# Expert loop: slot 3 in the first slot's buffer, slots 3 and 4 fetched before the router's tables, two low parts made by GpSimd

## The chip, the core and the metric

The kernel runs on one core of one Trainium2 chip. The metric is the device time of one execution in microseconds (us), as the median of several runs.

## What is computed

Two transformer blocks over 512 tokens of width 1024, in float32. The first block has sparse latent attention, a chunked gated MLP and a mixture of experts; the second has dilated attention, forgetting attention and SwiGLU layers. The change touches the mixture of experts only:

```python
def hier_moe(h, ...):
    # group = top 1 of 4, then top 2 of its 8 experts; comb = gate weights, zero elsewhere
    y = zeros_like(h)
    for e in range(32):
        he = silu(h @ w_gate[e]) * (h @ w_up[e])      # 1024 -> 256
        y = y + comb[:, e:e + 1] * (he @ w_down[e])   # 256 -> 1024
    return y
```

## The kernel before, in words

The 1024 pairs of token and expert are sorted by expert into slots of up to 64 rows. A slot belongs to one expert. The first 32 slots are those of experts 0 to 31, in order, whatever the router finds; experts with more than 64 rows get further slots behind them. Here 36 slots are worked off, one after the other.

Products are made in a split form. A weight w is parted into a high part (rounded by ScalarE) and a low part (w minus the high part, a subtraction of two operands in SBUF); TensorE multiplies by both. For a slot, ScalarE makes `up_high` and VectorE `up_low` (line 2553) from the gate and the up weights in two steps (q = 0 gate, q = 1 up), each 128x2048. They are double buffered by the slot's parity. `m_low` counts the low parts: 1 and 2 are slot 0's, 3 and 4 slot 1's, 2j + 1 and 2j + 2 slot j's.

Raw weights come by transfers of 1 MB for gate, up and down, issued in program order by SyncE (lines 672, 675, 678). Slot 0's stand in `w_first`; all later slots use a ring of two buffers, odd slots in one and even slots in the other. The gate and up transfers of slot j wait until slot j - 2's low parts are made, its down transfer until slot j - 2's down product is done. Slots 0, 1 and 2 are fetched before the router; slots 3 and 4 follow once the router's tables are there (`rt_tables`), since `next_up` reads the expert's number from a table.

The router runs between the rows' norm and the loop, at about 395 to 412 us: VectorE does some 60 small steps (compare, multiply, reduce; most wait for the step before), with short products on TensorE between. It writes `slot_rows` (which rows a slot has) and the trip count. GpSimd then gathers each slot's rows by indirect transfers and scatters the results. `keep_clock` issues idle products on TensorE so that its clock is kept.

In a period of the loop VectorE adds the two halves of the gated product (line 2280), multiplies by the Silu, copies the down product of an earlier slot out of PSUM, and makes the two low parts of the next slot with a step for its rows between. The first of these periods stand written out ahead of the loop.

Before the loop VectorE makes slot 0's gate low part ahead of the router (at 391.8), its up low part right behind the tables (at 412.0), and both of slot 1's behind the first rows. GpSimd clears the gather buffer `xg` at 369 and then waits for `slot_rows`.

## Time and profile before

| | us |
|---|---|
| median of 3 runs | 2420.23 |
| lowest, highest | 2414.74, 2420.58 |
| the profiled execution | 2420.1 |
| its span, first to last instruction | 2418.2 |

| engine | busy us | share of the span |
|---|---|---|
| TensorE | 2305.2 | 95% |
| VectorE | 979.5 | 41% |
| ScalarE | 968.9 | 40% |
| GpSimd | 945.1 | 39% |

All times inside the kernel are in us from the start of the span. PE is TensorE, DVE VectorE, ACT ScalarE, POOL GpSimd, SP SyncE; SPq is SyncE's issuing of a transfer. The shares hold for the whole kernel; the stage that the change touches runs from about 395 to 730 us, and there the windows, the waits and the timeline have to be read for themselves. `L2553` is line 2553 of the kernel. A row of the timeline gives start, duration, engine, line, operation, output and inputs, shapes and count.

### The profile page before, as it was taken

To read this page: it belongs to the slowest core of one execution; us is meant where nothing else is said; L and a number is where in the kernel's file an instruction comes from. 1 tells how busy PE (TensorE), PEld (TensorE's weight loads), DVE (VectorE), ACT (ScalarE), POOL (GpSimd) and SP (SyncE) were. 2 spreads that over 40 slices of the span, in tenths; PEclk is the share of its full clock that TensorE was granted. 3 is DMA by queue.
4 is the path that set the end of the run, shared out by engine and by line. 5 is a ranking of instruction groups with operands and counts; after the bars stand their busy time and mean duration, and the time that the engine had idled before them with its cause. 6 is when DMAs were issued, how large, how long until landed. Compare 5 with 4: busy or idle time off the path is not lost.

```text
span 2418.2 us, 31089 instructions
## 1 busy us (share of the span) xinstructions
PE 2305.2 (95%) x11628; PEld 1872.7 (77%) x11628; DVE 979.5 (41%) x1631; ACT 968.9 (40%) x1611; POOL 945.1 (39%) x757
## 2 busy tenths in 40 slices
PE   7999998888888999999998899999999999999998
PEld 6886786444446998899987778888878887888887
DVE  4377445888884233363335621111321124211113
ACT  3344523666663344343343432222344444322223
POOL 4441241535552433333332145454432222544542
PEclk9999999999999999999999999999999999999999
DMA  5521146999983422312322133333232211233332
GB/s 180 170 76 47 40 156 226 356 391 399 387 322 116 146 84 96 102 53 70 105 86 73 36 92 101 99 93 105 88 106 87 70 53 53 87 105 91 101 98 85
DMA packets 210268, 316.25 MB, mean 131 GB/s; under 512 B 20640, under 2 KB 140192, under 8 KB 200304
## 3 DMA queue, kind: packets, MB, share of 16 engines
q1 hardware_dynamic: 202416, 301.98, 36.5%
q0 software_dynamic: 7744, 12.76, 1.6%
q8 instruction: 76, 1.25, 0.2%
q14 instruction: 32, 0.26, 0.0%
HBM read 300.89 MB, written 22.71 MB: 134 GB/s over the span
## 4 chain that ended last, share of the span: by engine, by line
PE 77%; DVE 6%; issue 5%; DMA 5%; ACT 3%; POOL 2%; SPq 1%; DVEq 0%; ACTq 0%; POOLq 0%
PE bank L873 21%; PE bank L875 21%; PE bank L874 21%; DMA w_ring<-in_w_gate 4%; PE bank L1493 2%; PE bank L1125 2%; POOL w_low L3036 2%; DVE up_low L2553 2%; PE bank L912 1%; PE bank L1104 1%; PE bank L1470 1%; PE bank L1115 1%; PE bank L1480 1%; ACT up_high L1984 1%; PE bank L1297 1%
## 5 line engine op out<-in xcount | busy, mean ns | idle before, releaser
L3036 POOL TENSOR_TENSOR w_low<-raw,w_high 128x512 fp32r<-128x512 f32 x568 | 743.4, 1340 | 1180.7 <-ACT w_high L1730 1148.8
L873 PE MATMUL bank<-h_high,w_high 128*128 128x512 f32 x1088 | 430.8, 396 | 2.3 <-DVE h_low L2297 2.3
L875 PE MATMUL bank<-h_high,w_low 128*128 128x512 f32 x1088 | 425.5, 391 | 0.0
L874 PE MATMUL bank<-h_low,w_high 128*128 128x512 f32 x1088 | 425.1, 391 | 0.0
L1730 ACT ACTIVATE w_high<-raw 128x2048 fp32r<-128x2048 f32 x145 | 276.9, 1909 | 246.8 <-PE bank L875 233.8
L873 PE MATMUL bank<-w_high,h_high 128*128 128x512 f32 (+2 forms) x832 | 328.2, 394 | 13.6 <-ACT qk L2065 4.1
L875 PE MATMUL bank<-w_high,h_low 128*128 128x512 f32 (+2 forms) x832 | 312.3, 375 | 0.0
L874 PE MATMUL bank<-w_low,h_high 128*128 128x512 f32 (+2 forms) x832 | 312.3, 375 | 0.0
L873 PEld LDWEIGHTS bank<-h_high,w_high 128*128 128x128 f32 x1088 | 205.3, 189 | 47.1 <-DVE h_low L2297 6.1
L875 PEld LDWEIGHTS bank<-h_high,w_low 128*128 128x128 f32 x1088 | 205.0, 188 | 43.6
L874 PEld LDWEIGHTS bank<-h_low,w_high 128*128 128x128 f32 x1088 | 205.3, 189 | 40.4
L873 PEld LDWEIGHTS bank<-w_high,h_high 128*128 128x128 f32 x832 | 204.9, 246 | 29.3 <-DVE h_low L2297 4.6
L875 PEld LDWEIGHTS bank<-w_high,h_low 128*128 128x128 f32 x832 | 204.9, 246 | 12.3
L874 PEld LDWEIGHTS bank<-w_low,h_high 128*128 128x128 f32 x832 | 206.1, 248 | 10.7
L2553 DVE TENSOR_TENSOR up_low<-w_ring,up_high 128x2048 fp32r<-128x2048 f32 x70 | 160.2, 2290 | 25.2 <-ACT up_high L1984 24.4
L2277 DVE TENSOR_TENSOR gu<-silu,bank 128x512 f32<-128x512 f32 x44 | 30.3, 688 | 321.4 <-ACT silu L2177 321.4
L2177 ACT ACTIVATE silu<-bank 128x512 f32<-128x512 f32 x44 | 26.3, 598 | 333.1 <-PE bank L875 333.1
L2280 DVE TENSOR_TENSOR X<-bank,X 128x512 f32<-128x512 f32 x96 | 65.8, 690 | 210.5 <-PE bank L875 210.2
L1984 ACT ACTIVATE up_high<-w_ring 128x2048 fp32r<-128x2048 f32 x70 | 133.8, 1913 | 23.9 <-DMA w_ring<-in_w_gate 20.7
L2119 ACT ACTIVATE dsc<-dsc,nmx 128x128 f32<-128x128 f32 (+1 forms) x192 | 81.8, 428 | 138.9 <-DVE nmx L2910 138.9
L873 PE MATMUL bank<-w_high,act_high 128*128 128x512 f32 x352 | 136.9, 389 | 0.0
L874 PE MATMUL bank<-w_low,act_high 128*128 128x512 f32 x352 | 136.9, 389 | 0.0
(378 smaller groups left out, 3371.3 us busy)
## 6 DMA issues: line engine op xcount, KB each, us to landing
raw<-in_ffn_w_gu SPq DMA_DIRECT2D x88, 512.0 KB, 4.5
raw<-in_a_w_in SPq DMA_DIRECT2D x72, 512.0 KB, 4.6
w_ring<-in_w_gate SPq DMA_DIRECT2D x35, 1024.0 KB, 10.1
w_ring<-in_w_up SPq DMA_DIRECT2D x35, 1024.0 KB, 12.3
w_ring<-in_w_down SPq DMA_DIRECT2D x35, 1024.0 KB, 9.2
raw<-in_ffn_w_down SPq DMA_DIRECT2D x40, 512.0 KB, 4.6
raw<-in_w_in SPq DMA_DIRECT2D x34, 512.0 KB, 4.6
raw<-in_b_w_in SPq DMA_DIRECT2D x24, 512.0 KB, 4.6
```

The source lines that it names most:

```text
L873: pe.matmul(out, sta[0], mov[0], start=start, stop=False)
L874: pe.matmul(out, sta[0], mov[1], start=False, stop=False)
L875: return pe.matmul(out, sta[1], mov[0], start=False, stop=stop)
L1125: last = pe.matmul(G[qt % 2][:, h * DH:(h + 1) * DH], pt_[:, u % deep, kt * P:(kt + 1) * P], v_[:, kt, h * DH:(h + 1) * DH], start=(kt == ...
L1493: last = pe.matmul(G[t % 2][:, h * DH:(h + 1) * DH], dPT[:, u % 3, o:o + P], dV[:, v % 2, kt, h * DH:(h + 1) * DH], start=(z == 0), stop=( ...
L1730: act.activation(w_high[:, slot, :], raw[:, slot, :], ACT.Copy).then_inc(high_done, 1)
L1984: act.activation(up_high[:, b, :, FE * q:FE * q + FE], ring[:, q, :].rearrange("p (k n) -> p k n", k=KD), ACT.Copy).then_inc(m_high, 1)
L2119: last = act.activation(dsc[:, u % 3, e * w:(e + 1) * w], dsc[:, u % 3, e * w:(e + 1) * w], ACT.Exp, bias=nmx[:, col:col + 1], accum_out=s ...
L2277: return dve.tensor_tensor(out=out, in0=x, in1=y, op=ALU.mult)
L2280: return dve.tensor_tensor(out=out, in0=x, in1=y, op=ALU.add)
L2553: dve.tensor_tensor(out=up_low[:, b, :, FE * q:FE * q + FE], in0=ring[:, q, :].rearrange("p (k n) -> p k n", k=KD), in1=up_high[:, b, :, F ...
L3036: last = pool.tensor_tensor(out=w_low[:, slot, cols], in0=raw[:, slot, cols], in1=w_high[:, slot, cols].bitcast(F32), op=ALU.subtract)
```

## The change

Slot 3 goes to `w_first`, which slot 0 leaves; the ring's two buffers change places (slots 1, 4, 6, 8, ... in ring 0, slots 2, 5, 7, ... in ring 1). SyncE issues the gate and up transfers of slots 3 and 4 by their fixed expert numbers before it waits for the tables, each behind a low part that frees its place; slots 3, 4 and 5 have issues of their own, and the broadcast of `final_norm_g` comes behind slot 6's. GpSimd makes the up low part of slot 0 and the gate low part of slot 1, each in four subtractions of 128x512, while the router runs; VectorE then makes one low part (slot 1's up) after the tables. The router's scratch tiles move to other addresses (two of them over `xg`, with a wait for its clearing), four semaphores of the router become two counting ones, and the first slots of TensorE's and ScalarE's loops are written out.

```diff
-    row_hot = at("row_hot", 93, [P, 2 * NT, R])
-    slot_hot = at("slot_hot", 95, [P, 2 * NT, SLOTS])
+    row_hot = at("row_hot", 29, [P, 2 * NT, R])
+    slot_hot = at("slot_hot", 31, [P, 2 * NT, SLOTS])
...
-    w_ring = [at("w_ring0", AR, [P, 3, 2048]), at("w_ring1", AR + 56, [P, 3, 2048])]
+    w_ring = [at("w_ring0", AR + 56, [P, 3, 2048]), at("w_ring1", AR, [P, 3, 2048])]
...
-        gate(w_ring[1], 1, m_up[1][0])
-        up(w_ring[1], 1, m_up[1][1])
+        gate(w_ring[0], 1, m_up[0][0])
+        up(w_ring[0], 1, m_up[0][1])
...
-                gate(w_ring[0], 2, m_up[0][0])
-                up(w_ring[0], 2, m_up[0][1])
-                down(w_ring[0], 2, m_dn[0])
+                gate(w_ring[1], 2, m_up[1][0])
+                up(w_ring[1], 2, m_up[1][1])
+                down(w_ring[1], 2, m_dn[1])
         sp.wait_ge(rt_out, NT)
-        down(w_ring[1], 1, m_dn[1])
+        down(w_ring[0], 1, m_dn[0])
+        sp.wait_ge(m_low, 1)
+        gate(w_first, 3, m_gate3)
+        sp.wait_ge(m_low, 2)
+        up(w_first, 3, m_up3)
+        sp.wait_ge(m_low, 3)
+        gate(w_ring[0], 4, m_up[0][0])
+        sp.wait_ge(m_low, 4)
+        up(w_ring[0], 4, m_up[0][1])
...
-        next_up(3, 1)
-        next_up(4, 0)
         sp.wait_ge(m_down, 1)
+        down(w_first, 3, m_dn3)
+        sp.wait_ge(m_low, 5)
+        gate(w_ring[1], 5, m_up[1][0])
+        sp.wait_ge(m_low, 6)
+        up(w_ring[1], 5, m_up[1][1])
+        sp.wait_ge(m_down, 2)
+        down(w_ring[0], 4, m_dn[0])
+        next_up(6, 0)
+        sp.wait_ge(m_low, 8)
         sp.dma_start(gw1[:, :], a["final_norm_g"].partition_broadcast(P)).then_inc(gains_loaded, 16)
-        with sp.Fori(2, n_less) as i:
+        with sp.Fori(3, n_less) as i:
             next_down(2 * i - 1, 1)
             next_up(2 * i + 1, 1)
             next_down(2 * i, 0)
...
-        down(0, 0, 1, lambda: rows_come(1, 2))
-        with pe.Fori(1, n_trips) as i:
-            turn_rows(2 * i + 1, 1)
-            up(2 * i, 0, 2 * i - 1)
-            down(2 * i - 1, 1, i, lambda: rows_come(0, i + 2))
...
+        down(0, w_first, m_first, 48, lambda: rows_come(1, 2))
+        turn_rows(3, 1)
+        up(2, 0, 1)
+        down(1, w_ring[0], m_dn[0], 16, lambda: rows_come(0, 3))
...
+        down(3, w_first, m_dn3, 16, lambda: rows_come(0, 4))
...
+        with pe.Fori(2, n_less) as i:
...
+        act.wait_ge(rt_tables, 1)
         rows_high(0, 0)
-        act.wait_ge(rt_tables, 1)
...
-        period(1, 1, 1)
-        with act.Fori(1, n_less) as i:
-            period(2 * i, 0, i + 1)
-            period(2 * i + 1, 1, i + 1)
+        period(1, 1, w_ring[1], m_up[1], 1)
+        period(2, 0, w_first, [m_gate3, m_up3], 1)
+        period(3, 1, w_ring[0], m_up[0], 2)
+        with act.Fori(2, n_less) as i:
...
+        dve.wait_ge(m_idx, 6)
         step(dve.tensor_tensor(out=row_hot[:, :, :],
...
         dve.drain().then_inc(m_y, 1)
-        dve.wait_ge(m_part, 8)
-        up_part(w_first, 0, 1)
+        dve.wait_ge(m_low, 3)
+        up_next(1, 1, 1, w_ring[0])
         rows(0, 0)
         rows(1, 1)
-        up_next(1, 1, 0)
-        up_next(1, 1, 1)
-        period(1, 1)
+        period(1, 1, ring=w_ring[1])
...
-        period(2, 0, 0)
+        period(2, 0, 0, w_first)
...
         pool.memset(xg[:, :, :], 0.0).then_inc(m_idx, 6)
...
+        def up_low_part(ring, b, q):
+            for k in range(0, KD, 2):
+                part = (slice(0, P), b, slice(k, k + 2), slice(FE * q, FE * q + FE))
+                last = pool.tensor_tensor(out=up_low[part],
+                                          in0=ring[:, q, FE * k:FE * k + 2 * FE].rearrange("p (k n) -> p k n", k=2),
+                                          in1=up_high[part].bitcast(F32), op=ALU.subtract)
+            last.then_inc(m_low, 1)
+
+        pool.wait_ge(m_part, 8)
+        pool.wait_ge(m_low, 1)
+        up_low_part(w_first, 0, 1)
+        pool.wait_ge(rt_out, NT)
+        pool.wait_ge(m_high, 1)
+        up_low_part(w_ring[0], 1, 0)
         pool.wait_ge(rt_slots, 1)
```

## Rows read from the trace of the kernel before

**Rows 1.** Page, part 4: shares of the chain by line
```profile
PE bank L873 21%; PE bank L875 21%; PE bank L874 21%; DMA w_ring<-in_w_gate 4%; PE bank L1493 2%; PE bank L1125 2%; POOL w_low L3036 2%; DVE up_low L2553 2%; PE bank L912 1%; PE bank L1104 1%; PE bank L1470 1%; PE bank L1115 1%; PE bank L14
```

**Rows 2.** Windows of the expert stage: window, length, busy us (count) by engine, PEclk, DMA share, GB/s
```profile
core 0: us, PE busy (x) PEld busy (x) DVE busy (x) ACT busy (x) POOL busy (x), PEclk, DMA share, GB/s
395.00:405.00 10.00, 8.26 (x30) 3.87 (x29) 8.94 (x37) 5.71 (x6) 0.00 (x0) 0.90 0.92 366
405.00:412.00 7.00, 4.62 (x20) 2.98 (x21) 4.87 (x19) 0.00 (x0) 1.20 (x2) 0.50 0.00 1
420.00:440.00 20.00, 17.66 (x89) 10.78 (x88) 17.98 (x22) 12.64 (x14) 6.08 (x6) 1.00 0.77 262
440.00:460.00 20.00, 17.85 (x84) 10.55 (x82) 19.08 (x23) 14.23 (x17) 14.93 (x11) 1.00 0.97 378
500.00:600.00 100.00, 83.44 (x382) 48.05 (x380) 86.07 (x93) 61.68 (x68) 51.68 (x46) 0.97 1.01 397
```

**Rows 3.** Waits of ScalarE, 464 to 710 us: line, awaited, us, times, longest
```profile
ACT up_high L1984 <- DMA w_ring<-in_w_gate: 20.7, 23, 1.9
```

**Rows 4.** SyncE issues of ring weights by tile, each with its time to landing
```profile
L672 SPq DMA_DIRECT2D w_ring<-in_w_gate x1: 346/346/346, 421.7 to 421.7; - x1
...
DMA to landing us min/median/max: 4.9/4.9/4.9
...
L678 SPq DMA_DIRECT2D w_ring<-in_w_down x1: 383/383/383, 438.8 to 438.8; - x1
...
DMA to landing us min/median/max: 5.4/5.4/5.4
...
L678 SPq DMA_DIRECT2D w_ring<-in_w_down x1: 391/391/391, 454.6 to 454.6; - x1
...
DMA to landing us min/median/max: 7.6/7.6/7.6
...
L672 SPq DMA_DIRECT2D w_ring<-in_w_gate x1: 333/333/333, 455.9 to 455.9; - x1
...
DMA to landing us min/median/max: 10.2/10.2/10.2
```

**Rows 5.** Timeline of GpSimd and VectorE: the same subtraction with and without GpSimd at work
```profile
1032.69 5.04 POOL L3036 TENSOR_TENSOR w_low<-raw,w_high 128x512 fp32r<-128x512 f32 x4 [17.85 <-ACT w_high L1730]
...
1034.11 1.15 DVE L2853 TENSOR_TENSOR top<-m,msm 128x8 f32<-128x8 f32 x1
1035.30 1.23 DVE L2283 TENSOR_TENSOR mw<-msm,top 128x24 f32<-128x24 f32 x1
...
1053.14 0.18 DVE L2283 TENSOR_TENSOR mw<-msm,top 128x24 f32<-128x24 f32 x1
```

**Rows 6.** Tile w_first and the timeline of VectorE, ScalarE and GpSimd through the router
```profile
L1955 ACT ACTIVATE up_high<-w_first x8: 618/622/622, 387.4 to 394.8; 128x512 fp32r<-128x512 f32 x8
...
395.52 0.17 DVE L2578 TENSOR_TENSOR goh<-logit,rv 128x16 f32<-128x16 f32 x1
...
398.44 0.19 DVE L2573 TENSOR_REDUCE rv<-el 128x4 f32<-128x32 f32 x1
...
411.61 0.16 DVE L2677 CAST trips<-posf 1x3 int32<-1x3 f32 x1
...
410.49 1.01 POOL L3088 DMA_INDIRECT xg<-d_rows,slot_rows  x1 [39.68 <-DVE slot_rows L2666]
```

**Rows 7.** Timeline of VectorE and ScalarE in the first slots of the expert loop
```profile
419.22 4.49 DVE L2553 TENSOR_TENSOR up_low<-w_ring,up_high 128x2048 fp32r<-128x2048 f32 x2
...
423.62 0.74 DVE L2280 TENSOR_TENSOR gated<-lower,bank 64x256 f32<-64x256 f32 x2
...
422.60 1.28 ACT L2007 ACT_TABLE_LOAD   x1
...
440.39 0.74 DVE L2280 TENSOR_TENSOR gated<-lower,bank 64x256 f32<-64x256 f32 x2
...
448.21 0.74 DVE L2280 TENSOR_TENSOR gated<-lower,bank 64x256 f32<-64x256 f32 x2
```

More of the change, by code:

```diff
@@ L197, in two_blocks_kernel @@
     x_turn = at("x_turn", 93, [P, KD, T])
-    row_hot = at("row_hot", 93, [P, 2 * NT, R])
-    slot_hot = at("slot_hot", 95, [P, 2 * NT, SLOTS])
-    cut7 = at("cut7", 97, [P, 2 * NT, T // R - 1])
-    slote = at("slote", 97.25, [1, SLOTS])
-    cnt = at("cnt", 97.5, [1, 1])
-    over = at("over", 97.625, [P, 2 * NT])
-    own = at("own", 97.6875, [P, 2 * NT])
-    cut = at("cut", 97.75, [P, 2 * NT])
-    posf = at("posf", 97.8125, [P, 2 * NT])
-    row_of = at("row_of", 97.875, [P, 2 * NT])
-    starts = at("starts", 98, [P, NE])
-    more = at("more", 98.125, [NE, T // R - 1])
-    more_sum = at("more_sum", 98.1875, [NE, 1])
-    more_wide = at("more_wide", 98.25, [NE, P])
+    row_hot = at("row_hot", 29, [P, 2 * NT, R])
+    slot_hot = at("slot_hot", 31, [P, 2 * NT, SLOTS])
+    cut7 = at("cut7", AR + 28.375, [P, 2 * NT, T // R - 1])
+    slote = at("slote", AR + 28.625, [1, SLOTS])
+    cnt = at("cnt", AR + 28.84375, [1, 1])
+    over = at("over", AR + 28.875, [P, 2 * NT])
+    own = at("own", AR + 28.90625, [P, 2 * NT])
+    cut = at("cut", AR + 28.9375, [P, 2 * NT])
+    posf = at("posf", AR + 28.96875, [P, 2 * NT])
+    row_of = at("row_of", AR + 29, [P, 2 * NT])
+    starts = at("starts", AR + 29.03125, [P, NE])
+    more = at("more", AR + 29.1875, [NE, T // R - 1])
+    more_sum = at("more_sum", AR + 29.21875, [NE, 1])
+    more_wide = at("more_wide", AR + 29.25, [NE, P])
     logit = at("logit", AR + 24, [P, NT, 36])
@@ L1239, in _ @@
         keep_clock(4, TB[0])
-        pe.wait_ge(rt_both, 1)
+        pe.wait_ge(rt_ready, 1)
         for q in range(NT):
             last = pe.matmul(SB[1][0:NE, 0:8], both[:, q, :], ones_r[:, 0:8], start=(q == 0), stop=(q == NT - 1))
-        last.then_inc(rt_cnt, 1)
+        last.then_inc(rt_counted, 1)
         for t in range(NT):
@@ L1298, in up, with down @@
             last.then_inc(m_gu, 1)
-        def down(j, b, uses, come=None):
+        def down(j, ring, loaded, count, come=None):
             pe.wait_ge(m_het, j + 1)
-            if isinstance(j, int) and j == 0:
-                pe.wait_ge(m_first, 48)
-                w = w_first[:, 2, :].rearrange("p (k n) -> p k n", k=2)
-            else:
-                pe.wait_ge(m_dn[b], 16 * uses)
-                w = w_ring[b][:, 2, :].rearrange("p (k n) -> p k n", k=2)
+            pe.wait_ge(loaded, count)
+            w = ring[:, 2, :].rearrange("p (k n) -> p k n", k=2)
             pe.wait_ge(m_y, j + 1)
@@ L1985, in up_part, with up_next @@
                            ACT.Copy).then_inc(m_high, 1)
-        def up_next(j, b, uses, q):
-            act.wait_ge(m_up[b][q], 16 * uses)
+        def up_next(j, b, ring, loaded, uses, q):
+            act.wait_ge(loaded[q], 16 * uses)
             if q == 0 and (not isinstance(j, int) or j >= 2):
                 act.wait_ge(m_gu, j - 1)
-            up_part(w_ring[b], b, q)
+            up_part(ring, b, q)
         def rows_high(j, b):
@@ L2601, in _ @@
         step(add(oh_sum[:, :, :], oh[:, 0, :, :], oh[:, 1, :, :]))
-        spread(both[:, :, :], oh_sum[:, :, :]).then_inc(rt_both, 1)
+        spread(both[:, :, :], oh_sum[:, :, :]).then_inc(rt_ready, 1)
         for k in range(2):
@@ L2696, in inner, with up_next @@
             mul(he[:, :], sg[:, :], gated[:, FE:2 * FE]).then_inc(m_he, 1)
-        def up_next(j, b, q):
+        def up_next(j, b, q, ring):
             dve.wait_ge(m_high, 2 * j + q - 1)
-            up_part(w_ring[b], b, q)
+            up_part(ring, b, q)
         def out(j, b, i):
@@ L2707, in out, with period @@
             dve.tensor_copy(y_out[:, b, 512:1024], G[3][R:2 * R, :]).then_inc(m_y, 1)
-        def period(j, b, i=None):
+        def period(j, b, i=None, ring=None):
+            ring = w_ring[1 - b] if ring is None else ring
             inner(j - 1, 1 - b)
@@ L2712, in period @@
                 out(j - 2, b, i)
-            up_next(j + 1, 1 - b, 0)
+            up_next(j + 1, 1 - b, 0, ring)
             rows(j + 1, 1 - b)
-            up_next(j + 1, 1 - b, 1)
+            up_next(j + 1, 1 - b, 1, ring)
         dve.drain().then_inc(m_y, 1)
-        dve.wait_ge(m_part, 8)
-        up_part(w_first, 0, 1)
+        dve.wait_ge(m_low, 3)
+        up_next(1, 1, 1, w_ring[0])
         rows(0, 0)
         rows(1, 1)
-        up_next(1, 1, 0)
-        up_next(1, 1, 1)
-        period(1, 1)
+        period(1, 1, ring=w_ring[1])
         dve.wait_ge(rt_tables, 1)
```

69 lines of the change are left out of this document (40 added, 29 removed).

## Prediction

> **What bounds the kernel now.** I read the page's chain of waits first: three quarters of it is TensorE in the dense layers, and the expert stage shows up as 4% on the gate weights of the ring [rows 1]. The change touches only the router and the expert loop, 395 to 730 us, so I read that stage by its own views. In the windows the DMA share is 0.92 in the router's first ten us, 0.00 from 405 to 412, 0.77 from 420 to 440, 0.97 to 460, and 1.01 in the loop [rows 2]. The waits of ScalarE say the same: behind 464 us it waited 23 times for a slot's gate weights, 20.7 us in all [rows 3]. So the loop has two speeds. Up to slot 6 VectorE sets the pace, busy 19.08 us of 20 [rows 2], one slot in 7.8 us (gated halves at 440.39 and 448.21 [rows 7]). From slot 7 on the transfers do: its gate weights were issued at 455.9 and landed 10.2 us later, at 466.1 [rows 4]. The end of the loop is the end of that stream of transfers, and what ran dry before is what could be won: the queue is empty while the router works out its tables, which end at 411.61 + 0.16 = 411.8 [rows 6], and the first ring issue after them is at 421.7 [rows 4].
>
> **The change, part by part.**
> *Slots 3 and 4 ahead.* Their experts are numbers 3 and 4 whatever the router finds, so the transfers need no table. The first slot's buffer is free for slot 3 when its two low parts are made, ring 0 (now slot 1's) for slot 4 when slot 1's are. Four transfers of 1 MB move forward: gate 3 to 395, up 3 and gate 4 to GpSimd's two ends (below, 400.7 and 405.8), up 4 behind VectorE's one low part after the tables. At the 397 GB/s of the loop [rows 2] one takes 1.049 MB / 397 = 2.64 us. They are hidden in the empty stretch. Yet the head start does not last: slot 6 still needs slot 4's low parts gone, as before, so the third buffer helps once. I follow the queue, first with the router's end unmoved. Down 3, gate 5, up 5 go out at 429 to 431, when before gate 4 and up 4 did; down 4 at 438; gate 6 and up 6 at slot 4's low parts (the second ends where the gated half at 448.21 starts [rows 7], the first some 2.8 us before, at 445.4); then the broadcast of the norm gains, 0.5 MB, which used to run in a gap behind up 4 and now stands in the way for 1.3 us. Up 6 lands alone, 4.9 us after its issue as gate 3 did [rows 4], at 453.1; the gains at 454.5. Down 5 waits for slot 3's down product and is issued at 454.5, as before [rows 4], so the queue is empty again there. It then lands after 5.4 us, the time of down 3 on an empty queue [rows 4], so at 459.9 or, with the start of the chain 0.2 us earlier, 459.7; before it landed at 454.6 + 7.6 = 462.2. That is 2.5 us won. Gate 7, one transfer behind, lands at 462.4 instead of 466.1: 3.7 us. From here on the stream is full in both kernels, slot for slot the same, and the lead stays. I take 3.1 us, the middle of 2.5 and 3.7. The other ends: 0 if the queue's order eats it, and 4 x 2.64 = 10.6 us if all four transfers that moved ahead come off the end.
> *VectorE's work moved.* After the tables it did one low part of slot 0 and, from 419.22, both of slot 1 (4.49 us) before the first gated half at 423.62 [rows 7]. Now it does one, of slot 1, right after the tables. But ScalarE starts to load its Silu table at 422.60 for 1.28 us [rows 7], so the activation can't start before 423.88, and the next conversion follows it. The cover is the table load: 4.49 us of work go, about 0.2 us of time come back. Ends 0 and 1.0 (423.62 - 422.60).
> *GpSimd's two low parts.* It had nothing to do from 371 to 410 (idle 39.68 before its first gather [rows 6]), so its own time costs nothing. Each low part is four subtractions of 128x512, 5.04 us for four [rows 5]. They begin when ScalarE's last first part is done, 394.8 + 0.62 = 395.4 [rows 6], say 395.5, and run with a small gap to about 405.7. Exactly there VectorE runs the router's chain, dependent step by dependent step. Here the trace has a price: with four such GpSimd subtractions running from 1032.69 on, VectorE's 128x8 and 128x24 subtractions took 1.15 and 1.23 us; the same 128x24 one with GpSimd idle took 0.18 [rows 5]. Each waited out the GpSimd instruction in front of it, and GpSimd was hardly slowed (5.04 / 4 = 1.26). So one dependent two-operand step of VectorE passes per GpSimd instruction. The Trainium skill's page "SBUF — State Buffer", section "Who interferes with whom", states this as an exclusive lock held for a whole instruction, taken when VectorE has two SBUF inputs and GpSimd reads SBUF, never by a reduction; it speaks against this placement, and the trace agrees with 1.15 and 1.23 us.
> Counting: from 395.52 the router's steps are, by the kernel's text, compare, multiply, (reduce), compare, multiply, (two reduces), compare, multiply, (reduce), compare, combine, and then the reduce at 398.44 [rows 6]. Eight two-operand steps, eight GpSimd subtractions: the last gets through when GpSimd ends, 395.5 + 8 x 1.26 + 0.1 = 405.7, takes 0.2, and the reduce of 398.44 starts at 405.9. The router's chain is 7.4 us late, and everything behind it: tables at 419.2. Ends: 0 (the small steps slip through) and, if VectorE in turn stretches GpSimd's instructions, some 10.
> *Rest.* The merged semaphores count the same events; the wait of VectorE for the cleared gather buffer was met at 371; ScalarE's wait for the tables before the first rows stands 4 us ahead of those rows; SyncE passes nothing that is due while it waits for low parts, since its next issues need the tables anyway; the unrolled slots and the turned parity cost nothing. One answer: 0, with 0.5 either way.
>
> **Sum.** Made against the profiled execution, 2420.1 us with a span of 2418.2; the median of three is 2420.2, so the difference can be added to either. +7.4 - 0.2 - 3.1 = +4.1. Everything from the tables to about slot 9 shifts whole, since nothing there waits for a transfer any more, and the stream that is full afterwards starts 4 us later. 2420.2 + 4.1 = 2424.3 us. A measurement of this kernel tells about 0.3%, 7.3 us, from no change (the three runs lie 5.8 us apart), so this counts as the same.
>
> **The rivals.**
> *A, the forecast,* the hold of 7.4 us outweighs the lead of 3.1: 2424.3. For it: [rows 5], and the count of eight against eight. Chance 0.60.
> *B, no hold.* VectorE's steps are short, and [rows 5] has only two of them beside GpSimd. If most slip between two GpSimd instructions, the router keeps its time: -3.1 - 0.2, 2416.9. Against it: every router step depends on the one before. Chance 0.17.
> *C, the lead is kept whole.* If the stream, not VectorE, would be the bound from slot 2 on, all four transfers would count: 2420.2 - 10.6 + 7.4 = 2417.0 with the hold (chance 0.05), 2409.6 without it (0.04). Against it: VectorE's 19.08 of 20 us [rows 2] says that the slots cannot run faster than 7.8, so the queue must empty once more.
> *D, slower.* VectorE's steps also stretch GpSimd's instructions, each by its own length, and the router meets the pair on more steps; the delay is 10 us or more, and TensorE, idle at the granted clock of 0.50 as in 405 to 412 [rows 2], starts the first slots with half speed, 1 to 2 us: 10.3 - 3.3 + 1.5 = +8.5, 2428.7. It decides from a delay of 10.6 us on, where +7.3 is reached. Against it: 5.04 us for four beside a busy VectorE. Chance 0.14.
>
> **How the numbers follow.** Likeliest is A, 2424.3. The range must hold 8 in 10: from B's and C's 2416.9, less 1 for the spread of the runs, to D's 2428.7: 2416 to 2429. Outside stay C without the hold (0.04) and some tails of D. Faster by over 0.3% (under 2413.0): only C without the hold, 0.04. Slower by over 0.3% (above 2427.5): most of D and a tail of A, 0.13. The same: 0.83.
>
> **What would show it.** In the profile after: GpSimd with eight subtractions from 395.5 to about 405.7; the router's multiplies and compares at 1.1 to 1.3 us instead of 0.2 between; the table cast at about 419 instead of 411.61; ring or first-buffer transfers in the stretch 405 to 412; the queue empty again before down 5; ScalarE's first long wait for gate weights at slot 9 or later instead of 7, and its sum well under 20.7 us. Router steps at 0.2 us mean B. A down 5 that finds a full queue means that the lead was sized wrongly. A loop end that moves by another amount than the tables less 3 us means that the stream is not what sets the end.

## The result, and the profile after it

The changed kernel took 2424.72 us (median of 11 runs) where the kernel before, on the same chip, took 2418.72 (11 runs); the ratio is 1.0021, with an interval of 1.0012 to 1.0030. Times the 2420.2 us of before, that is +5.1 us; the forecast was +4.1. It is a small loss, and it lies inside the 0.3% that the prediction called the same.

The profiled execution took 2423.33 us with a span of 2421.5, before 2420.1 and 2418.2. That difference of 3.3 us is the sum of four, and only one, the +4.4 us of the table below, belongs to the change. Everything up to the router ran 3.15 us earlier in this execution (its first group compare starts at 392.37, before at 395.52 [rows 6]). Behind the stage, up to 943 us, it gained another 1.1 us. And a stretch that the change doesn't touch, from 1266 to 1408 us, ran 3.1 us longer, with two spells of half clock on TensorE, from 1290 and from 1303 us on, where before had one from 1301 on. So I count the landmarks of the router and of the expert loop from the router's first group compare, to the loading of the layer behind the loop ("end" below):

```
us behind the first group compare   before   after   difference
the reduce of 398.44 [rows 6]          2.92     9.93   +7.01
the routing one-hots (both)            4.25    11.27   +7.02
slot_hot                              11.23    18.85   +7.62
tables (the cast of trips)            16.09    23.72   +7.63
first Silu (slot 0)                   28.54    35.33   +6.79
Silu of slot 9                       106.32   111.39   +5.07
Silu of slot 20                      203.28   207.52   +4.24
end of the stage                     335.54   339.92   +4.38
```

First the router. These are VectorE's steps in the changed kernel (start, duration, engine, line, operation, tiles) from the first group compare to the reduce that before stood at 398.44:

```profile
392.37 1.27 DVE L2601 TENSOR_TENSOR goh<-logit,rv 128x16 f32<-128x16 f32 x1
393.68 1.19 DVE L2300 TENSOR_TENSOR goh<-goh,cst 128x16 f32<-128x16 f32 x1
394.91 0.17 DVE L2596 TENSOR_REDUCE rv<-goh 128x4 f32<-128x16 f32 x1
395.11 0.99 DVE L2604 TENSOR_TENSOR goh<-goh,rv 128x16 f32<-128x16 f32 x1
396.13 1.30 DVE L2300 TENSOR_TENSOR r<-logit,goh 128x128 f32<-128x128 f32 x1
397.47 0.38 DVE L2596 TENSOR_REDUCE el<-r 128x32 f32<-128x128 f32 x1
397.88 0.19 DVE L2596 TENSOR_REDUCE rv<-el 128x4 f32<-128x32 f32 x1
398.10 0.51 DVE L2601 TENSOR_TENSOR oh<-el,rv 128x32 f32<-128x32 f32 x1
398.64 1.18 DVE L2300 TENSOR_TENSOR oh<-oh,cst 128x32 f32<-128x32 f32 x1
399.86 0.19 DVE L2596 TENSOR_REDUCE rv<-oh 128x4 f32<-128x32 f32 x1
400.08 0.96 DVE L2604 TENSOR_TENSOR oh<-oh,rv 128x32 f32<-128x32 f32 x1
401.08 1.18 DVE L2614 SCALAR_TENSOR_TENSOR el<-oh,el 128x32 f32<-128x32 f32 x1
402.30 0.19 DVE L2596 TENSOR_REDUCE rv<-el 128x4 f32<-128x32 f32 x1
...
416.09 0.16 DVE L2701 CAST trips<-posf 1x3 int32<-1x3 f32 x1
```

and these are GpSimd's over the same time:

```profile
392.34 4.95 POOL L3105 TENSOR_TENSOR up_low<-w_first,up_high 128x512 fp32r<-128x512 f32 x4 [24.68 <-ACT up_high L1976]
397.25 4.97 POOL L3105 TENSOR_TENSOR up_low<-w_ring,up_high 128x512 fp32r<-128x512 f32 x4
```

Eight steps with two operands are long and all reduces are short (0.17 to 0.38 us). Eight GpSimd subtractions run from 392.34 to 402.22, and the reduce of 402.30 starts as the last one ends. One step ended with each subtraction; where reduces took up part of a subtraction's time (the compare at 398.10, 0.51 us), only the rest was waited for.

Then the transfer queue. The stretches of the changed kernel (length, busy us and count by engine, PEclk, DMA share, GB/s), and after them one stretch of the kernel before over the same times:

```profile
core 0: us, PE busy (x) PEld busy (x) DVE busy (x) ACT busy (x) POOL busy (x), PEclk, DMA share, GB/s
392.00:402.00 10.00, 3.35 (x8) 1.14 (x6) 9.55 (x14) 5.25 (x4) 9.66 (x8) 0.86 1.00 390
402.00:409.00 7.00, 5.01 (x20) 4.18 (x21) 5.91 (x24) 0.31 (x2) 0.22 (x1) 0.50 0.94 398
409.00:416.00 7.00, 6.36 (x22) 3.29 (x21) 5.13 (x18) 0.00 (x0) 1.01 (x1) 0.50 0.03 14
...
446.00:451.00 5.00, 5.00 (x27) 2.83 (x28) 4.95 (x5) 3.86 (x5) 3.29 (x2) 1.00 0.33 90
451.00:458.00 7.00, 6.29 (x27) 3.32 (x26) 6.68 (x9) 5.38 (x6) 5.35 (x5) 1.00 0.98 382
458.00:460.00 2.00, 2.00 (x16) 1.71 (x15) 2.00 (x2) 0.00 (x0) 2.00 (x1) 1.00 0.56 105
```

```profile
446.00:451.00 5.00, 4.27 (x25) 2.71 (x22) 4.71 (x8) 2.59 (x4) 4.00 (x3) 1.00 1.00 387
```

The stretch beside the router, where before had 0.00 from 405 to 412 [rows 2], is filled at 0.94 to 1.00 until 409. What was moved there is missing later: from 446 to 451 the share is 0.33 (before 1.00, in a loop that had begun 3.6 us earlier), and there is a second gap at 458 to 460, ahead of down 5. SyncE's issues show down 5 and gate 7 at the same distance from the first Silu as before (30.5 and 31.8 us; before 454.6 and 455.9 [rows 4]):

```profile
402.25 0.33 SPq L670 DMA_DIRECT2D w_ring<-in_w_gate  x1
418.87 0.33 SPq L673 DMA_DIRECT2D w_ring<-in_w_up  x1
433.32 0.38 SPq L676 DMA_DIRECT2D w_first<-in_w_down  x1
433.75 0.47 SPq L670 DMA_DIRECT2D w_ring<-in_w_gate  x1
...
449.20 0.34 SPq L670 DMA_DIRECT2D w_ring<-in_w_gate  x1
451.97 0.34 SPq L673 DMA_DIRECT2D w_ring<-in_w_up  x1
452.37 0.42 SPq L739 DMA_DIRECT2D gw<-in_final_norm_g  x1
458.19 0.38 SPq L676 DMA_DIRECT2D w_ring<-in_w_down  x1
459.52 0.33 SPq L670 DMA_DIRECT2D w_ring<-in_w_gate  x1
```

ScalarE's first long wait for gate weights (the end of its conversions' idle time, in brackets) is now for gate 8, at 477.33. The conversion of gate 7, which before waited until 466.1 [rows 4], waited for no transfer:

```profile
477.33 1.92 ACT L2005 ACTIVATE up_high<-w_ring 128x2048 fp32r<-128x2048 f32 x1 [1.15 <-DMA w_ring<-in_w_gate]
```

Its waits for gate weights from 464 to 720 us (line, awaited, us, times, longest) come to 18.8 us, against 20.7 in [rows 3]:

```profile
ACT up_high L2005 <- DMA w_ring<-in_w_gate: 18.8, 24, 2.0
```

So from the first Silu to the end of the stage the changed kernel needs 304.59 us and before 307.00: the loop is 2.4 us shorter, behind a router that is 7.6 us longer. The lead arises at one place. The Silus of slots 1 to 4 stand where they stood, counted from the first one (slot 0's, at 424.06 before and at 427.70 after), slot 5's is 0.14 us ahead, and slot 6's is 1.5 us ahead: 49.58 us behind the first one before, 48.06 after. These are slot 6's Silus, before and after:

```profile
473.64 0.42 ACT L2007 ACTIVATE sg<-gated 64x256 f32<-64x256 f32 x1 [2.38 <-DVE gated L2280]
```

```profile
475.76 0.42 ACT L2028 ACTIVATE sg<-gated 64x256 f32<-64x256 f32 x1 [2.39 <-DVE gated L2303]
```

TensorE's clock is not the reason. The kernel before had three spells of half clock in its loop, 3.4 us each, from 485, 522 and 567 us on, and the changed kernel had none; but the first of them comes behind slot 6, and over none of the three did the lead grow.

### The profile page after: what moved, and what is told of

It is laid out like the page before. It is cut to its first block, busy times and chain, and to the rows that moved or that the text cites. A ratio compares the mean times of both kernels' runs of the same rounds, so it can differ in the third digit from the quotient of the medians.

```text
span 2421.5 us, 31064 instructions
## 1 busy us (share of the span) xinstructions
PE 2300.7 (95%) x11628; PEld 1871.4 (77%) x11628; DVE 980.9 (41%) x1629; ACT 968.8 (40%) x1611; POOL 954.5 (39%) x765
## 3 DMA queue, kind: packets, MB, share of 16 engines
q8 instruction: 77, 1.26, 0.2%
## 4 chain that ended last, share of the span: by engine, by line
PE 78%; issue 6%; DVE 5%; DMA 5%; ACT 3%; POOL 2%; SPq 1%; DVEq 0%; POOLq 0%; ACTq 0%
PE bank L886 21%; PE bank L888 21%; PE bank L887 21%; DMA w_ring<-in_w_gate 4%; PE bank L1514 2%; PE bank L1138 2%; POOL w_low L3059 2%; PE bank L925 1%; PE bank L1117 1%; PE bank L1491 1%; DVE up_low L2576 1%; PE bank L1128 1%; PE bank L1501 1%; PE bank L1322 1%; PE bank L1310 1%
## 5 line engine op out<-in xcount | busy, mean ns | idle before, releaser
L887 PEld LDWEIGHTS bank<-h_low,w_high 128*128 128x128 f32 x1088 | 204.9, 188 | 40.1
L2576 DVE TENSOR_TENSOR up_low<-w_ring,up_high 128x2048 fp32r<-128x2048 f32 x67 | 153.4, 2290 | 23.2 <-ACT up_high L2005 22.7
L2005 ACT ACTIVATE up_high<-w_ring 128x2048 fp32r<-128x2048 f32 x68 | 130.0, 1912 | 21.6 <-DMA w_ring<-in_w_gate 18.8
```

Source lines behind the costliest of these rows:

```text
L887: pe.matmul(out, sta[0], mov[1], start=False, stop=False)
L2005: act.activation(up_high[:, b, :, FE * q:FE * q + FE], ring[:, q, :].rearrange("p (k n) -> p k n", k=KD), ACT.Copy).then_inc(m_high, 1)
L2576: dve.tensor_tensor(out=up_low[:, b, :, FE * q:FE * q + FE], in0=ring[:, q, :].rearrange("p (k n) -> p k n", k=KD), in1=up_high[:, b, :, F ...
```

## The experiments

The theory was the forecast's: the router is held by GpSimd's subtractions (theory H), and the loop is shorter by the lead of the transfer queue (theory L). The rivals are these: the router is late for another reason (transfers beside it, GpSimd at work in any form); the lead comes from the third buffer's order and not from the early transfers; the lead is capped by something that can be moved. The diffs are against the changed kernel unless said. All lengths below are counted as in the table above: "tables" and "end" behind the first group compare, "loop" from the first Silu to the end.

```
kernel             reduce   tables  first Silu    end    loop
before               2.92    16.09    28.54     335.54  307.00
after                9.93    23.72    35.33     339.92  304.59
e1_dve_low           2.92    16.10    28.89     332.90  304.01
e2_no_ahead          9.93    22.91    39.56     344.05  304.49
e3_memset            2.92    16.10    27.71     333.16  305.45
e4_one_part          6.86    20.65    32.52     337.42  304.90
e5_fine              3.91    19.83    31.89     337.55  305.66
e6_gains_late        2.92    15.28    27.52     331.28  303.76
e7_down_early        2.92    16.10    29.11     332.94  303.83
e8_rows_first        9.93    22.94    33.32     337.58  304.26
e9_two_products      2.92    15.29    27.70     332.84  305.14
```

The sections below follow in the order e1 to e5, e8, e6, e7, e9. Each row is one profiled execution. The changed kernel, e1, e3, e4 and e5 issue the same transfers and run the same program from the first Silu on, and their loops are 304.01 to 305.66 us long; e6 and e9 are alike in the same way, with 303.76 and 305.14. So a difference of less than about 1.6 us between two of these loops shows nothing. All ten are 1.3 to 3.2 us shorter than the one profile of before, and in all ten slot 6's Silu stands 48.05 to 48.23 us behind the first, where before it stood at 49.58: the lead itself is real.

### Without GpSimd's part

```diff
-        dve.wait_ge(m_low, 3)
-        up_next(1, 1, 1, w_ring[0])
+        dve.wait_ge(m_part, 8)
+        up_part(w_first, 0, 1)
         rows(0, 0)
         rows(1, 1)
+        up_next(1, 1, 0, w_ring[0])
+        up_next(1, 1, 1, w_ring[0])
...
-        pool.wait_ge(m_part, 8)
-        pool.wait_ge(m_low, 1)
-        up_low_part(w_first, 0, 1)
-        pool.wait_ge(rt_out, NT)
-        pool.wait_ge(m_high, 1)
-        up_low_part(w_ring[0], 1, 0)
```

> The change with its GpSimd part undone: VectorE makes both low parts after the tables, as in the kernel before; the early transfers stay, each behind the same low part. My theory (the hold by GpSimd costs, the lead pays): from the router's first group compare to the tables' last cast 16.1 us as before, not 23.7; every later landmark about 7 us earlier than in the changed kernel; the lead of about 2.5 to 3 us is kept whole, because from slot 3's down transfer on all issues hang on the slots' own pace, not on when up 3 and gate 4 came. The stretch from the first compare to the start of the loading of y_in, 335.5 us before and 339.9 after, becomes 332.5 to 333.5; the kernel 2 to 4 us faster than before. Rival (no hold, the router was late for another reason such as the clock or the moved scratch tiles): tables still near 23.7 and no gain against the changed kernel. Rival (the lead needs gate 4 at 402): the stretch is 335.5, as before.

It took 2416.91 us (11 runs), before 2418.96 (21 runs): ratio 0.9991 [0.9980, 1.0001], or 2.2 us faster with an interval that just takes in no change. The end at 332.90 is inside the forecast of 332.5 to 333.5. The router is back: tables at 16.10, before 16.09, changed kernel 23.72. Three router steps, long above, are short again:

```profile
392.24 0.17 DVE L2601 TENSOR_TENSOR goh<-logit,rv 128x16 f32<-128x16 f32 x1
392.45 0.17 DVE L2300 TENSOR_TENSOR goh<-goh,cst 128x16 f32<-128x16 f32 x1
...
393.07 0.29 DVE L2300 TENSOR_TENSOR r<-logit,goh 128x128 f32<-128x128 f32 x1
```

The loop stays short, 304.01 us. So all 7.6 us of the router's delay are due to GpSimd's two low parts, and the loop's gain has nothing to do with them. One thing in it I had not looked for: up 3, gate 4 and up 4 go out here 18.8, 26.4 and 28.6 us behind the first compare (changed kernel 4.9, 9.9 and 26.5), since their low parts come later, and the loop is as short as ever. That speaks against the forecast's account of the lead; the next run and the one with the rows first bear on it.

### Without the early transfers

```diff
         down(w_ring[0], 1, m_dn[0])
+        sp.wait_ge(rt_tables, 1)
         sp.wait_ge(m_low, 1)
```

> The change with its early transfers undone: SyncE waits for the tables before gate 3, all else as changed, GpSimd's two low parts too. My theory: tables stay at 23.7 us behind the first compare; the lead goes, so the stretch to y_in is 335.5 + 6.8 = 342.3 us instead of 339.9, and the kernel about 7 us slower than before, 2.4 slower than the changed one. Rival (the early transfers bring nothing): 339.9 us and the same time as the changed kernel. Rival (they get in the way of the row gathers): faster than the changed kernel.

It took 2428.77 us (4 runs): ratio 1.0041 [1.0025, 1.0056] against before. It is slower than the changed kernel, but not where I expected it: the loop is 304.49 us long, as short as with the transfers early. What was lost lies ahead of the loop, 4.2 us later at the first Silu. The turns of the first gathered rows show it:

```profile
417.36 0.70 PE L1288 MATMUL bank<-cst,xg 64*128 64x64 f32 x8 [0.99 <-DMA xg<-d_rows,slot_rows]
423.34 1.11 PE L1288 MATMUL bank<-cst,xg 64*128 64x64 f32 x8 [5.28 <-DMA xg<-d_rows,slot_rows]
```

while in the changed kernel both go together:

```profile
419.66 1.21 PE L1287 MATMUL bank<-cst,xg 64*128 64x64 f32 x16 [1.00 <-issue]
```

The gathers of rows here (before the same view has 2.8, 2.9 and 6.7 us):

```profile
DMA to landing us min/median/max: 2.8/6.6/8.1
```

Four transfers of 1 MB were issued at once behind the tables, and the rows of slots 1 and 2 landed beside them (DMA share 0.79 from 416 to 432 where the changed kernel has 0.30). So the early transfers are worth something only against this version, because they keep the queue clear when the rows come. They are not what shortens the loop.

### GpSimd at work, but reading nothing

This kernel leaves out two low parts (the second of slot 0, the first of slot 1): GpSimd sets them to zero instead of subtracting, so that it works in the same place and the products run over zeros.

```diff
-                last = pool.tensor_tensor(out=up_low[part],
-                                          in0=ring[:, q, FE * k:FE * k + 2 * FE].rearrange("p (k n) -> p k n", k=2),
-                                          in1=up_high[part].bitcast(F32), op=ALU.subtract)
+                last = pool.memset(up_low[part].bitcast(F32), 0.0)
```

> The change, but GpSimd clears the low parts in place of subtracting: eight instructions of the same shape that write SBUF and read nothing from it (slot 0's up low part and slot 1's gate low part are left out of the products). If the hold comes from both engines reading two operands of SBUF, as I hold, VectorE's small steps beside them take their 0.17 to 0.29 us and the tables come at 16.1 us. Rival (any GpSimd instruction holds VectorE): each step beside one waits for its end, and the tables are late by about the sum of the eight instructions less the reductions.

It ran once, in 2414.56 us, so its time says little; its trace is what counts. GpSimd writes beside the same router steps, and none of those with two operands is longer than 0.29 us:

```profile
391.28 1.92 POOL L3105 MEMSET up_low<- 128x512 f32 x4 [24.65 <-ACT up_high L1976]
```

```profile
391.34 0.17 DVE L2601 TENSOR_TENSOR goh<-logit,rv 128x16 f32<-128x16 f32 x1
...
392.17 0.29 DVE L2300 TENSOR_TENSOR r<-logit,goh 128x128 f32<-128x128 f32 x1
```

Tables at 16.10. GpSimd writing the same tile at the same place holds nobody, so neither its work as such nor its writes are the cause; what is left is that a subtraction reads SBUF, and that it is another operation. This agrees with the Trainium skill's page "SBUF — State Buffer", section "Who interferes with whom", by which a VectorE instruction with two SBUF inputs contends with a GpSimd instruction that reads SBUF, and not with one that only writes. A memset takes 0.48 us and a subtraction of the same size 1.24 us, so the two differ in length too; subtractions of 0.45 us come below, and they hold steps.

### Half of GpSimd's part

```diff
-        dve.wait_ge(m_low, 3)
-        up_next(1, 1, 1, w_ring[0])
+        dve.wait_ge(m_low, 2)
         rows(0, 0)
         rows(1, 1)
+        up_next(1, 1, 0, w_ring[0])
+        up_next(1, 1, 1, w_ring[0])
...
-        pool.wait_ge(rt_out, NT)
-        pool.wait_ge(m_high, 1)
-        up_low_part(w_ring[0], 1, 0)
```

> Half of the GpSimd part: it makes slot 0's up low part (four subtractions) and VectorE both of slot 1's. One held step per GpSimd instruction gives four held steps: 4 x 1.23 us less the four steps' own time and the reductions between (0.17 + 0.17 + 0.17 + 0.17 + 0.29 and gaps), so the second part's reduce starts about 3.8 us late, and the tables at 16.1 + 3.8 = 19.9 us. With the whole lead kept the stretch to y_in is 335.5 + 3.8 - 2.7 = 336.6. Rival (the delay is a fixed cost of starting GpSimd): near 7.6 late or 0.

It took 2418.81 us (10 runs): ratio 1.0000 [0.9991, 1.0009]. Four subtractions, four held steps, and the hold ends with them:

```profile
395.59 4.95 POOL L3106 TENSOR_TENSOR up_low<-w_first,up_high 128x512 fp32r<-128x512 f32 x4 [24.67 <-ACT up_high L1976]
```

```profile
399.39 1.30 DVE L2300 TENSOR_TENSOR r<-logit,goh 128x128 f32<-128x128 f32 x1
...
401.35 0.19 DVE L2601 TENSOR_TENSOR oh<-el,rv 128x32 f32<-128x32 f32 x1
```

The reduce is 3.94 us late, the changed kernel's 7.01: the price goes with the number of GpSimd instructions. The tables are 4.56 us late, 0.6 more than the reduce, as in the changed kernel. The forecast had 3.8 us for both: right for the reduce, and without the 0.6 behind it, which is taken up further down.

### The same work in small pieces

```diff
-            for k in range(0, KD, 2):
-                part = (slice(0, P), b, slice(k, k + 2), slice(FE * q, FE * q + FE))
-                last = pool.tensor_tensor(out=up_low[part],
-                                          in0=ring[:, q, FE * k:FE * k + 2 * FE].rearrange("p (k n) -> p k n", k=2),
-                                          in1=up_high[part].bitcast(F32), op=ALU.subtract)
+            for k in range(KD):
+                for h in range(2):
+                    c0 = FE * q + P * h
+                    part = (slice(0, P), b, k, slice(c0, c0 + P))
+                    last = pool.tensor_tensor(out=up_low[part], in0=ring[:, q, FE * k + P * h:FE * k + P * h + P],
+                                              in1=up_high[part].bitcast(F32), op=ALU.subtract)
```

> The change with GpSimd's 8 subtractions of 128x512 cut into 32 of 128x128. If each GpSimd instruction lets one dependent two-operand step of VectorE through and holds the next, a step now waits at most about 0.35 us: some 11 us of GpSimd work with about 0.3 us of waiting at each of 15 to 18 two-operand steps, so the tables 4 to 5.5 us late instead of 7.6. Rival (GpSimd keeps the pair of ports over its queue of instructions): 7 us late or more.

It took 2422.68 us (8 runs), before 2417.41 (35 runs): ratio 1.0013 [1.0001, 1.0025]. A router step is now longer by 0.33 us at most (`row_of`, 0.50 us and not 0.17), so the reduce is only 1.0 us late. But the 32 instructions last longer together, 14.9 us instead of 9.9,

```profile
395.65 6.86 POOL L3107 TENSOR_TENSOR up_low<-w_first,up_high 128x128 fp32r<-128x128 f32 x16 [24.67 <-ACT up_high L1976]
402.46 7.71 POOL L3107 TENSOR_TENSOR up_low<-w_ring,up_high 128x128 fp32r<-128x128 f32 x15
```

(the view ends ahead of the last of the 32, which ran until 410.6) and hold more of the steps that follow; the tables are 3.7 us late instead of 7.6, a little under the 4 to 5.5 of the forecast. So the hold of one step gets shorter with the GpSimd instruction, as the theory has it, and the rival (a hold over the whole queue of GpSimd, 7 us or more) is out. The hold also works the other way here: most of the 32 pieces took 0.45 to 0.51 us, but four took 0.64 to 0.90 us, beside VectorE's larger steps (`r`, 128x256, and the two of `row_hot`, 128x512).

### Rows first, then the transfers

To see whether being early brings anything at all, SyncE waits ahead of gate 3 until the rows of slots 0 to 2 are turned (gate 3 goes out 32.1 us behind the first compare instead of at once):

```diff
         down(w_ring[0], 1, m_dn[0])
+        sp.wait_ge(m_turned, 3)
         sp.wait_ge(m_low, 1)
```

> The changed kernel with SyncE waiting, ahead of gate 3, until the rows of slots 0 to 2 are turned, so that no weights run beside the first row gathers and none is fetched before the tables. If the lead comes from the early transfers themselves, they are gone and the stretch from the router's first group compare to the loading of y_in grows from 339.9 us by the lead of some 2.6 to 342.5. My theory now, after the run in which VectorE made the low parts (gate 4 at 26.4 us behind the first compare as before, and yet the whole lead of 2.6): the lead comes from the third buffer alone, which lets gate 5 and up 5 follow slot 2's low parts instead of slot 3's. Then 339.9 to 340.5, and the first Silu at 35.3 as in the changed kernel, not at 39.6 as with all four transfers issued beside the gathers.

It took 2422.98 us (10 runs): ratio 1.0025 [1.0015, 1.0036], the changed kernel's 1.0021 within the interval. The loop is 304.26 us long. So the early transfers bring the loop nothing that these runs show: with all four late, and the rows out of their way, it is as short as with them early. The place of the first Silu was missed: 33.32 and not 35.3, since the tables came 0.8 us earlier (22.94 and not 23.72) and TensorE's idle products behind them took 3.70 us at full clock and not 4.92. With that the end is 337.58, while the runs' time is no better than the changed kernel's.

What is common to all versions with the short loop is the third buffer: gate 5 and up 5 follow slot 2's low parts, where before gate 4 and up 4 did, so the stream is one slot ahead when the loop starts. This is by elimination. No run keeps two buffers and has the rest of the change; that the lead shows at the same slot, 6, in all ten kernels speaks for it.

### The broadcast of the gains out of the way

From the version without GpSimd's part:

```diff
-        sp.wait_ge(m_low, 8)
-        sp.dma_start(gw1[:, :], a["final_norm_g"].partition_broadcast(P)).then_inc(gains_loaded, 16)
...
         next_down(2 * n_less2 + 3, 1)
+        sp.dma_start(gw1[:, :], a["final_norm_g"].partition_broadcast(P)).then_inc(gains_loaded, 16)
```

> VectorE makes both low parts, and the broadcast of the norm gains is issued behind the last slot's down transfer instead of behind slot 6's up. If the stream of transfers sets the end of the loop, 0.5 MB less in it is worth 0.524 / 397 = 1.3 us: the stretch to y_in 331.6 us instead of 332.9. Rival (the broadcast falls into an empty stretch of the queue, ahead of down 5): no change, 332.9.

It took 2413.09 us (10 runs): ratio 0.9989 [0.9978, 1.0000]. The loop is 303.76 us long against 304.01, where the forecast had counted 1.3 us less. Both values are inside the spread of such loops (e9, with the same transfers as this kernel, has 305.14), so what the broadcast costs isn't measured. The rival has the trace for it: without the broadcast the queue stands empty just there, ahead of down 5 (the row in the next section), so there was a gap that could take it up. The end came where the forecast had it (331.28, forecast 331.6), but not for its reason. Half of what makes this kernel end earlier than the one without GpSimd's part (332.90) is that its tables come 0.8 us sooner, since 16 list products took 1.13 us at full clock and not 1.95 at half.

### Down 5 earlier

```diff
         down(w_ring[0], 4, m_dn[0])
+        sp.wait_ge(m_down, 3)
+        down(w_ring[1], 5, m_dn[1])
         next_up(6, 0)
-        with sp.Fori(3, n_less) as i:
+        next_up(7, 1)
+        next_down(6, 0)
+        next_up(8, 0)
+        with sp.Fori(4, n_less) as i:
```

(against the kernel with the gains late)

> As the run before, and slot 5's down transfer is issued when slot 2's down product is done, which frees its place, not when slot 3's is: it goes into the stretch in which the queue is empty. One transfer of 1 MB less in the full stream, 2.64 us: the stretch to y_in about 329 us, the kernel 5 to 7 us (0.2 to 0.3%) faster than before. Rival (the stretch is bound by the slots by then, or gate 6 behind it comes late): 331.6 or more.

It took 2414.02 us (12 runs): ratio 0.9986 [0.9977, 0.9995]. With the gains late alone, the queue is empty ahead of down 5 (columns as above, DMA share next to last),

```profile
449.40:451.40 2.00, 2.00 (x16) 1.63 (x15) 2.00 (x2) 0.00 (x0) 2.00 (x1) 1.00 0.02 6
```

and here the same place of the loop, whose first Silu stands 2.6 us later in this execution, is full; what is left is a gap ahead of gate 6:

```profile
444.00:446.00 2.00, 2.00 (x15) 1.10 (x12) 2.00 (x1) 0.05 (x1) 1.99 (x1) 1.00 0.24 33
...
452.00:454.00 2.00, 2.00 (x15) 1.63 (x14) 2.00 (x2) 0.00 (x0) 2.00 (x1) 1.00 1.06 369
```

The Silu of slot 9 stands 74.75 us behind the first one, with the gains late alone 75.53. But the loop is 303.83 us long, as before this edit (303.76), and not 2.6 us shorter. A miss: the 0.8 us at slot 9 are about what e6 and e9, with the same transfers, differ by there (75.53 and 76.26), and the two kernels' ratios, 0.9986 and 0.9989, have intervals that cover each other. The edit also cost something. SyncE issues in order, so gate 6 now stands behind the wait for slot 2's down product: down 5 goes out 7.5 us sooner, counted from the first Silu (23.0 and not 30.5 us), but gate 6 goes out 2.6 us later (24.1 and not 21.5), as the rival had it. The Silus run about 7.8 us one from the next up to slot 7 in this kernel (before up to slot 4), and while they do, a stream that is ahead has no slot that could use it. How much each of the two takes from the 2.6 us isn't measured.

### Fewer idle products ahead of the first rows

TensorE runs idle products to keep its clock until the rows come, and the first rows' turn starts 1.0 us after the last of them in every kernel here. Against the kernel with the gains late:

```diff
         last.then_inc(rt_counted, 1)
-        keep_clock(4, TB[0])
+        keep_clock(2, TB[0])
         phase_mark()
         pe.wait_ge(rt_tables, 1)
```

> The kernel with both low parts on VectorE and the gains' broadcast late, and behind the router two idle products of TensorE in place of four. In all runs so far the first turn of rows starts 1.0 us after the end of those four products (19.4 + 1.0 = 20.4 us behind the first group compare in the kernel before, 26.3 + 1.0 in the changed one), not with the landing of the rows (2.8 us after their gather). If they, at half clock and up to 1.4 us each, are what ends the wait, two less let the turn start some 1.5 to 2.8 us earlier, at 17 to 18.5 us, bounded by the landing of the rows at about 18.8 + 0.1; the stretch to y_in 329.5 to 330 us in place of 331.3, the kernel 6 us (0.25%) faster than before. Rival (without them the half clock reaches into slot 0 and 1): the turn is earlier, but the first Silu is not.

It took 2416.26 us (11 runs), before 2418.02 (15 runs): ratio 0.9993 [0.9984, 1.0003]. The first turn starts 2.1 us earlier (17.17, not 18.31 + 1.00 = 19.31), but the second waits for its rows until 19.13, and the half clock, from 13.5 to 23.8, now reaches into slot 0: the first Silu stands at 27.70, not 27.52. So the rival came true. No gain; the products' end is not what the first slot waits for once they are two fewer.

## Why the prediction came out as it did

**The hold of the router** was right in kind, in count and nearly in size. Eight steps met eight subtractions, reduces passed, and the last step was through when GpSimd ended. Forecast 7.4 us, measured 7.0: a GpSimd instruction took 9.92 / 8 = 1.24 us and not 1.26 (0.2 us in eight), and the last step ended with the last subtraction, while I had given it 0.2 us behind it. Three runs carry it: without the subtractions the delay of the reduce is 0, with half of them 3.94, and with as many memsets in their place 0.

**What the forecast left out behind the hold:** 0.6 us between the routing one-hots and slot_hot (6.98 us before, 7.58 after). TensorE had half clock from 6.7 us behind the first compare for 17.1 us (before from 7.5 for 10.2), and the counting products, one of which the table work waits for, show it:

```profile
403.99 0.38 PE L1255 MATMUL bank<-ones_r,both 128*32 128x8 f32 x4 [8.64 <-DVE both L2300]
404.22 0.37 PE L1259 MATMUL bank<-both,tris_r 128*128 128x32 f32 x1
```

Before, these took 0.29 and 0.26 us. TensorE had been idle for 8.64 us ahead of them, waiting for the router. Rival D had this mechanism, with its time at 1 to 2 us in the first slots; it came as 0.6 in the router, and not in the slots.

**VectorE's moved work** was right. Forecast 0.2 us; the distance from ScalarE's copy of the products to the first Silu went from 2.08 to 1.90 us, and the Silu table load stands in it as forecast:

```profile
425.80 0.59 ACT L2026 ACTIVATE lower<-bank 64x512 f32<-64x512 f32 x1 [3.41 <-PE bank L1310]
426.41 1.28 ACT L2028 ACT_TABLE_LOAD   x1
427.70 0.42 ACT L2028 ACTIVATE sg<-gated 64x256 f32<-64x256 f32 x1
```

A further 0.66 us came back between tables and first Silu that was not forecast: the last idle products, which stand ahead of the first rows, took 4.92 us and not 5.66 at a clock that was half for less of them, and ended 2.6 us behind the tables instead of 3.3. That is the place of the clock's spells rather than the edit: over the kernels with these products unchanged, the distance was 1.3 to 3.6 us.

**The lead in the loop** is the step that failed in part. The queue's order was followed rightly: it ran empty before down 5, which went out at the same distance from the first Silu as before, and the loop was shorter. Three things were not right:
- The cause. I wrote that "the third buffer helps once", but counted the lead as what four transfers moved forward leave over, "hidden in the empty stretch". The runs without the early transfers have the same loop (304.49 and 304.26, changed kernel 304.59). What is left is the third buffer, which lets slot 5's weights go out where slot 4's did.
- The size, 3.1 us against 2.4. By slot: the Silu of slot 5 stands 0.14 us nearer to the first than before, that of slot 9 1.7, of slot 20 2.6, and the end 2.4. A lead of 3.7 at gate 7 was never there, and the forecast's own rows could have told. It let gate 7 land 2.64 us behind down 5, but in the kernel before the two landed at 462.2 and 466.1, 3.9 us apart, so one step was given two lengths and 1.2 us of lead came from nothing. Nobody waited for gate 7 in the changed kernel, so its landing is an estimate, from the packets of the weights' queue: 3.1 MB, three transfers, went through it between 467.8 us and gate 8's landing at 477.2. That puts gate 7's landing 40.1 us behind the first Silu, before 42.0: a lead of 1.9. Gate 8's conversion starts 49.6 us behind the first Silu, before 475.49 - 424.06 = 51.4, and the lead is 1.8 there. The 2.64 us are too short because the weights are not alone: in that same stretch 0.34 MB of rows and results moved beside them, and the three transfers took 9.4 us, 3.1 us each. "Slot for slot the same" did not hold either: the slots ran on at 7.8 us until slot 6 in the changed kernel, before until slot 4 (7.97 to slot 5). How much of the 0.7 us that the forecast was too high at the end is the spread between executions isn't known.
- The broadcast, which by the forecast "now stands in the way for 1.3 us". No run shows this cost: with it moved out the loop was 303.76 and 305.14 us long, with it in place 304.01.

**The sign on ScalarE** was off by one slot. I wrote that the first long wait for gate weights comes "at slot 9 or later instead of 7", and it came for gate 8. The sum of these waits, "well under 20.7", was 18.8: under it, not well under.

**The sum.** +7.0 for the hold, +0.6 for the products at half clock, -0.8 from tables to the first Silu (of it 0.2 forecast), -2.4 in the loop: +4.4 at the stage's end by the profile, +5.1 by the runs' ratio (its interval is +2.9 to +7.3). The forecast +4.1 is near both in part by luck, because its errors cancel: 0.4 too much for the hold and 0.6 left out ahead of the first Silu (which came back) on one side, 0.6 left out at the half clock and 0.7 too much for the lead on the other.

**The rivals.** B (no hold) is out by the router's rows. C (the lead whole, 10.6 us) is out by the loop's length, and by the queue that ran empty twice. D (a delay of 10 us or more, GpSimd stretched by VectorE) is out by the delay of 7.0 us and by 9.9 us for eight subtractions, 1.24 us each, where [rows 5] had 5.04 for four.

## What to carry to other kernels

An idle GpSimd is not free for a piece of work if that work reads SBUF beside a chain of short dependent steps on VectorE: count the two-operand steps of the chain that meet it, multiply by the length of one GpSimd instruction, and set that against what the move gains; here 7.0 us were paid to save VectorE 0.2. When a buffer is added and transfers are moved forward in one change, ask which of the two moves the limit, since filling an empty stretch of the queue gains nothing if the next slots can't run faster and it only empties later. Of these kernels those that leave the low parts on VectorE and keep the third buffer are at or under the time before: 0.9991 [0.9980, 1.0001] as they stand, 0.9989 [0.9978, 1.0000] with the gains late, and 0.9986 [0.9977, 0.9995], 3.4 us, with down 5 early as well. Only the last is clear of no change, and the three can't be told from each other.

## What the hardware showed that I had not expected

- The length of a held step is the same for 128x16 and for 128x128 elements (0.96 to 1.30 us, and 0.51 for one that met only the rest of an instruction): it ends with GpSimd's instruction. GpSimd was not slowed by these small steps (1.24 us each). A memset of the same 128x512 took about 0.5 us and held no step.
- Cutting a GpSimd subtraction into four pieces, 128x128 instead of 128x512, made the whole 1.5 times as long (14.9 against 9.9 us). A piece took 0.45 us at the least, not a quarter of 1.24; four of the 32 were held beside VectorE's steps of 128x256 and 128x512 and took 0.64 to 0.90 us, about 1.4 us more in all.
- Row gathers that land after 2.8 us on a quiet queue took up to 8.1 us beside four weight transfers of 1 MB, though they are issued by another engine.
- TensorE's spells at granted clock 0.50 behind the router lasted 3.4 to 17.1 us over all kernels. In the four kernels here with the router unheld, real low parts and the same TensorE program there (before, without GpSimd's part, gains late, down 5 earlier), the first began 5.5 to 11.5 us behind the first compare. With the router held alike, the first Silu stood at 35.3 us in the changed kernel, with 17.1 us of half clock, and at 33.3 with the rows first, with 13.7: a difference as large as the terms under study, though the two also differ in what the queue carries there.
